# Two blocks of a language model on one core: evictions and weight splits in another order, eight products moved into a recurrence

## The reference

```python
y_ssm = mamba2_mixer(z, xbc, dt_raw, ...) @ w_out_ssm      # four groups of 512 channels, each with its norm
y_lru = rglru_mixer(lru_x, lru_y, ...) @ w_out_lru         # 1280 channels, ten blocks of 128
h = h + (g_ssm * y_ssm + g_lru * y_lru) @ w_out            # g = sigmoid gates, 2 x 1024
h = h + (silu(gate) * up) @ w_ffn_out
return rmsnorm(h, norm_f_w)
# in rglru_mixer, per 128 channels:
u = causal_dwconv(xl); r, i = sigmoid(u@w_r + b_r), sigmoid(u@w_i + b_i)
a = exp(-8·r·softplus(-lam)); b = sqrt(-expm1(2·log a))·i·u
h_t = a_t·h_{t-1} + b_t;  out = h · gelu(yl)
```

## Time and profile before

| | |
|---|---|
| median of three runs | 3571.42 us (3570.7 to 3572.22) |
| profiled execution, its own time | 3571.62 us |
| its span | 3569.5 us |
| PE busy / DVE busy / ACT busy | 94% / 48% / 37% |
| granted TensorE clock, mean | 0.978 of 2.4 GHz |
| HBM read | 282.64 MB, 80 GB/s over the span |

### The profile page before, as it was taken

The page is one execution under the profiler, slowest core; times in us unless marked ns, Lnnn a source line. Parts: engine busy times, 40 slices in busy tenths (PEclk is TensorE's granted clock), DMA queues, the critical chain, the costliest instruction groups (busy, mean ns, idle before and its releaser), DMA issues.

```text
span 3569.5 us, 38933 instructions
## 1 busy us (share of the span) xinstructions
PE 3362.7 (94%) x15366; PEld 2724.7 (76%) x15366; DVE 1722.0 (48%) x2415; ACT 1334.0 (37%) x1894; POOL 30.6 (1%) x62
## 2 busy tenths in 40 slices
PE   8999989899999999998989999989998998999998
PEld 6888766677888888876667788877777876778887
DVE  4443444754443444344575444455445566544443
ACT  4332335343332333233534332345444456433322
POOL 0000000000000000000000000000000000000000
PEclk9999999999999999999999999999999999999999
DMA  4233211112333233321111223321211222333332
GB/s 141 95 97 94 93 65 53 33 54 89 97 94 99 91 99 92 98 90 59 59 33 60 88 96 92 99 70 45 74 48 48 84 84 69 96 97 100 95 93 67
DMA packets 107396, 288.05 MB, mean 81 GB/s; under 512 B 22912, under 2 KB 34176, under 8 KB 107216
## 3 DMA queue, kind: packets, MB, share of 16 engines
q1 hardware_dynamic: 91696, 278.70, 25.0%
q10 hardware_dynamic: 14208, 2.63, 0.4%
q0 software_dynamic: 1312, 4.25, 0.4%
HBM read 282.64 MB, written 2.88 MB: 80 GB/s over the span
## 4 chain that ended last, share of the span: by engine, by line
PE 76%; DVE 12%; ACT 8%; issue 3%; ACTq 1%; DMA 1%; DVEq 0%; SPq 0%
PE ps L729 23%; PE ps L731 22%; PE ps L730 22%; DVE wl L1841 3%; ACT wh L1298 3%; DVE mf L2025 2%; PE ps L738 2%; PE ps L1038 1%; PE ps L1033 1%; PE ps L1194 1%; DVE mf L2035 1%; PE ps L1176 1%; PE ps L1190 0%; ACTq L1575 0%; PE ps L743 0%
## 5 line engine op out<-in xcount | busy, mean ns | idle before, releaser
L1841 DVE TENSOR_TENSOR wl<-raw,wh 128x1024 fp32r<-128x1024 f32 (+2 forms) x581 | 652.5, 1123 | 1448.0 <-ACT wh L1298 1446.2
L729 PE MATMUL ps<-hnh,wh 128*128 128x512 f32 x2712 | 1095.7, 404 | 38.4 <-DVE mf L2488 12.7
L730 PE MATMUL ps<-hnl,wh 128*128 128x512 f32 x2712 | 1070.6, 395 | 0.0
L731 PE MATMUL ps<-hnh,wl 128*128 128x512 f32 x2712 | 1070.1, 395 | 0.0
L1298 ACT ACTIVATE wh<-raw 128x1024 fp32r<-128x1024 f32 (+2 forms) x581 | 567.4, 977 | 1055.9 <-PE ps L731 1024.8
L729 PEld LDWEIGHTS ps<-hnh,wh 128*128 128x128 f32 x2712 | 519.3, 191 | 170.4 <-issue 24.5
L731 PEld LDWEIGHTS ps<-hnh,wl 128*128 128x128 f32 x2712 | 518.0, 191 | 111.4
L730 PEld LDWEIGHTS ps<-hnl,wh 128*128 128x128 f32 x2712 | 519.6, 192 | 108.3 <-issue 4.0
L729 PE MATMUL ps<-mr,wh 128*128 128x512 f32 x1300 | 511.7, 394 | 18.6 <-DVE h L1967 8.2
L731 PE MATMUL ps<-mr,wl 128*128 128x512 f32 x1300 | 507.0, 390 | 0.0
L730 PE MATMUL ps<-mr,wh 128*128 128x512 f32 x1300 | 506.8, 390 | 0.0
(11 more groups left out here) (324 smaller groups left out, 2533.0 us busy)
## 6 DMA issues: line engine op xcount, KB each, us to landing
raw<-in_w_in SPq DMA_DIRECT2D x140, 512.0 KB, 3.5
raw<-in_ffn_w_gate SPq DMA_DIRECT2D x88, 512.0 KB, 3.5
raw<-in_ffn_w_up SPq DMA_DIRECT2D x88, 512.0 KB, 3.5
raw<-in_ffn_w_down SPq DMA_DIRECT2D x64, 512.0 KB, 3.5
raw<-in_w_ffn_in SPq DMA_DIRECT2D x44, 512.0 KB, 3.5
raw<-in_ffn_w_down SPq DMA_DIRECT2D x32, 384.0 KB, 3.1
raw<-in_w_out SPq DMA_DIRECT2D x32, 256.0 KB, 2.6
raw<-in_w_out_ssm SPq DMA_DIRECT2D x32, 256.0 KB, 2.6
```

Of the source, the lines that this page charges most:

```text
L729: self.e.matmul(out, ah, bh, start=start, stop=False, skip_group_check=shared)
L730: self.e.matmul(out, ah, bl, start=False, stop=False, skip_group_check=shared)
L731: m = self.e.matmul(out, al, bh, start=False, stop=stop, skip_group_check=shared)
L1841: self.e.tensor_tensor(lo[:, 0:n], k.raw[u % NRAW][:, 0:n], hi[:, 0:n].bitcast(F), ALU.subtract).then_inc(k.w_lo, 1)
```

## The change

Four edits. In `Vector`, `split` only notes the unit, and the instruction is issued by `flush`, which stands at the start of each step, unit and product and behind the evictions of `add_h`, `ffn_up` and `take_mix`. In `Program`, `rstd` on PE only notes that rows are due, and `root_rows` issues them two steps (6 matmuls) into the next product; where the stage's products are short, the first sum also moves behind the next product. The eight products of the last group go from ahead of `lru` into its iterations 1 to 3, the gate products from iterations 1 and 3 to 3 and 4, and slots in SBUF are dealt out anew. The table of `ssm_heads` has 45 steps in place of 43, with paces some 5% up, and 0.6 in place of 0.65 in `lru`.

```diff
-PACE_SSM_ROWS, PACE_SSM, PACE_LRU, PACE_LRU_END = 1.1, (1.1, 0.82, 0.82, 0.9), 0.65, 1.0
+PACE_SSM_ROWS, PACE_SSM, PACE_LRU, PACE_LRU_END = 1.1, (1.15, 0.86, 0.86, 0.95), 0.6, 1.0
+LRU_OUT, LRU_GATE = ((), (0, 1, 2), (3, 4, 5), (6, 7), ()), {3: 4, 4: 5}
-AT_CB, AT_TURN, AT_X = (0, 2, 2, 3), (6, 8), 8
-AT_ARG, AT_EXP, AT_W, AT_V = 6, 7, 8, 12
+AT_CB, AT_TURN, AT_X = (0, 2, 2, 3), (6, 10), (8, 9, 12, 13)
+AT_ARG, AT_EXP, AT_W, AT_V = 8, 9, 10, 14
...
 class Program:
     def step(self):
+        self.flush()
...
     def product(self, xs, ready, bank=None):
-        for _ in self.pieces(xs, ready, bank):
+        for n, _ in enumerate(self.pieces(xs, ready, bank)):
             self.beside()
+            if n == 1:
+                self.root_rows()
...
     def run_late(self):
-            if i >= 6:
-                self.sums(i - 6)
+            if i == 6 and not self.short:
+                self.sums(0)
             if i == 7:
+                if self.short:
+                    self.sums(0)
+                self.sums(1)
...
     def second(self, gain):
-        self.pace = 0.0
-        self.ssm_out(3)
         self.lru(gain)
...
     def lru(self, gain):
             for i in range(2):
                 self.product_h()
                 self.end_taps()
                 self.taps = self.lru_conv(p, i, u[i])
+                if outs:
+                    self.ssm_out_tile(3, outs.pop(0))
...
-            if p in (1, 3):
-                self.branch_acc(4 + p // 2)
+            for i in outs:
+                self.ssm_out_tile(3, i)
+            if p in LRU_GATE:
+                self.branch_acc(LRU_GATE[p])
...
 class Tensor:
     def rstd(self):
-        self.wait_ge(*k.rs_v.at(self.rs_n(), "cols"))
-        self.rows_of(k.ps[B_RSTD], k.rc, k.rs_p.up(self.rs_n(), "rows"))
+        self.rows_due = self.rs_n()
+    def root_rows(self):
+        k, n = self.k, self.rows_due
+        if n is not None:
+            self.rows_due = None
+            self.wait_ge(*k.rs_v.at(n, "cols"))
+            self.rows_of(k.ps[B_RSTD], k.rc, k.rs_p.up(n, "rows"))
...
 class Vector:
     def split(self, u):
+        self.flush()
+        self.unsplit = u
+    def flush(self):
+        if self.unsplit is not None:
+            u, self.unsplit = self.unsplit, None
+            self.split_unit(u)
+    def begin_product(self, bank):
+        self.flush()
+    def begin_unit(self):
+        self.flush()
...
     def add_h(self, i, scale):
                                     op0=ALU.mult, op1=ALU.add).then_inc(k.took, 1)
+        self.flush()
```

More of the change, by code:

```diff
@@ L182, in __init__ @@
         self.g_v = steps("g_v", in_order(
-            [(AT_X + i, f"x{i}") for i in range(4)], [(AT_ST + 2 + 4 * c, f"{n}{c}") for c in (1, 2) for n in "ds"],
+            four_at("x", AT_X), [(AT_ST + 2 + 4 * c, f"{n}{c}") for c in (1, 2) for n in "ds"],
             [(AT_OFF + 1 + 4 * c, f"m{c}") for c in range(1, 4)], [(AT_Y + 4 * c, f"y{c}") for c in range(1, 4)],
@@ L297, in __init__ @@
         self.gates_done, self.prepared = {}, []
+        self.short, self.rows_due, self.unsplit = False, None, None
         self.qk_took, self.v_took = {}, {}
@@ L345, in split @@
         pass
+    def flush(self):
+        pass
     def pieces(self, xs, ready, bank=None):
@@ L417, in add_h_all @@
         self.r += 1
+        self.short = len(xs) < 8
         for i in range(8):
@@ L655, in ssm_out, with ssm_out_tile @@
     def ssm_out(self, g):
+        for i in range(8):
+            self.ssm_out_tile(g, i)
+    def ssm_out_tile(self, g, i):
         k = self.k
[L657 to L660, removed]
+        xs = [k.pair(S_X[g % 2] + j, S_LO + j) for j in range(4)]
+        b = self.product(xs, lambda j: (k.g_a.at(g, f"hi{j}"), k.g_v.at(g, f"lo{j}")))
+        self.take_out(g, i, b)
         self.out_unit[g] = self.u
@@ L665, in lru @@
         self.lam()
-        y = [k.pair(L_Y + 2 * i, L_Y + 2 * i + 1) for i in range(10)]
+        y = [k.pair(s, s + 1) for at in L_Y for s in (at, at + 2)]
         uh = [k.pair(L_UH + 2 * i, L_UH + 2 * i + 1) for i in range(2)]
@@ L693, in lru @@
         gate = [k.slot(n) for n in L_GATE]
-        parts = [k.pair(L_UH + i, L_LO[i]) for i in range(8)]
+        parts = [k.pair(L_HI[i], L_LO[i]) for i in range(8)]
         for i in range(8):
@@ L1814, in scans @@
                     self.wait_ge(*V.at(p, f"y{i}"))
+                    if p >= 2:
+                        self.wait_ge(*k.acc_v.at((3, 3, 5)[p - 2], "set"))
+                    if p >= 3:
+                        self.wait_ge(k.unit_done, self.out_unit[3])
                     e.activation(y[2 * p + i][0][:, :], u[i][:, :], ACT.Copy).then_inc(*A.up(p, f"hi{i}"))
@@ L1835, in split, with flush, split_unit @@
     def split(self, u):
+        self.flush()
+        self.unsplit = u
+    def flush(self):
+        if self.unsplit is not None:
[5 more added lines that the diff above has]
+        self.flush()
+    def split_unit(self, u):
         k = self.k
@@ L1848, in start @@
         self.hn_last = 0
-        self.split(0)
+        self.split_unit(0)
         self.wait_ge(k.loaded["col"], 16)
@@ L1853, in start @@
             if i == 1:
-                self.split(1)
+                self.split_unit(1)
             self.wait_ge(*k.hn_a.at(i, "hi"))
@@ L1862, in start @@
             if i in (5, 7):
-                self.split((i - 1) // 2)
+                self.split_unit((i - 1) // 2)
         self.wait_ge(k.loaded["cst"], 32)
@@ L2382, in take_branch @@
         self.taken()
-        if n < 8:
-            self.wait_ge(self.k.unit_done, self.out_unit[2])
+        if n < 4:
+            self.wait_ge(*self.k.g_p.at(3, "n2"))
+        elif n < 8:
+            self.wait_ge(self.k.unit_done, self.out_unit[3])
         self.e.tensor_tensor(d[:, :], self.bank()[:, :], self.k.rs[:, :], ALU.mult).then_inc(self.k.took, 1)
@@ L2419, in ssm_heads @@
                 self.prepared.append(g)
-            if AT_X <= t < AT_X + 4:
-                i = t - AT_X
+            if t in AT_X:
+                i = AT_X.index(t)
                 bank = (st, off)[i % 2][:, :].rearrange("p (c q e) -> p c q e", c=4, q=2)
@@ L2691, in plan_units @@
             tiles(w, 0, 4)
-    tiles(ins["w_out_ssm_2"][3], 0, 8)
     for p in range(5):
-        tiles(w, 56 + 2 * p, 2)
+        outs = list(LRU_OUT[p])
+        for i in range(2):
+            tiles(w, 56 + 2 * p + i, 1)
+            if outs:
+                tiles(ins["w_out_ssm_2"][3], outs.pop(0), 1)
         tiles(w, 66 + 2 * p, 2)
-        if p in (1, 3):
-            tiles(w, 4 + p // 2, 1)
+        for i in outs:
+            tiles(ins["w_out_ssm_2"][3], i, 1)
+        if p in LRU_GATE:
+            tiles(w, LRU_GATE[p], 1)
         for m in ("lru_w_r_2", "lru_w_i_2"):
```

17 lines of the change are left out of this document (11 added, 6 removed).

## The result

The changed kernel takes 3430.09 us (median of four runs, 3421.9 to 3435.55) against 3571.56 us: a ratio of 0.9602, 95% interval 0.9583 to 0.9622. In a later measurement the same kernel took 3427.41 us.

A forecast was written before the change was run, and what follows sets the result against it. PE, busy for 94% of the span, was taken as the bound, with about 207 us of gaps. Gains of 29 + 20 + 17 + 22 + 9, 97 us, took the median of 3571.4 to 3475 us, range 3442 to 3522.

The forecast's parts named there:

- The prediction's own sign: Whole kernel: a mean granted clock near 0.985 would show the forecast right.
- 17 of 39.8 us, with the clock: State-space groups: deferred splits shorten short waits, 17 us gained including clock and the table's two steps; bounds 8 and 27.
- PE's products hide the steps: State-space table: two more steps help a transposition, within the 17 us, and are worth nothing by themselves elsewhere.
- Mixers' ends: End of each mixer: some 9 of 10.3 us of waits go, clock gives 2; 11 us, twice; bounds 7 and 13 each.
- Attention: Attention and heads: a quarter of 41.3 us of gaps goes, 10 us per layer, 20 in both; bounds 4 and 16 per layer.
- Recurrence: Recurrence: 20.7 us from earlier evictions, 3 from the eight moved products, 5 from clock; 29 us, bounds 15 and 37.
- The rivals' bound: Recurrence becomes DVE's: it cannot go under 190 us; at 210 it gains 9, not 29; total 3495 us, chance 0.10.
- The four other roots: Roots not counted elsewhere: later rows let PE work meanwhile, 5.4 us, with slow pieces 9 us together; bounds 5 and 12.
- Almost all gaps close: Rival, whole kernel: nearly all gaps go with their slow pieces, the upper bounds, 3438 us; chance 0.07.
- The next link: Rival: chains through ACT return the gain at the next wait; half of the sum, 3523 us; chance 0.20.
- DVE's splits come too late: Rival, recurrence and mixer's end: delayed splits cost PE up to 0.68 us each; 3611 us at 200 paid splits; chance 0.03.
- The drain at the mixers' ends: Rival: DVE needs 5.6 us per tile, so order does not matter there; 22 us less gain, 3497 us; chance 0.02.

## Why the prediction missed

**The sign and most of the waits were right, most of the clock was missing.** DVE's idle time ahead of splits fell from 1446 to 603 us; the lone evictions that held PE in the recurrence cost 2.6 us in place of 12.7; feed-forwards kept their length (358.4 us, the dip behind the root gone); PE's wait for the reciprocal is 0.7 us, a little under the 0.8 to 0.9 expected; the granted clock is 0.988. The 141.2 us by which the spans differ can be parted, since both kernels run the same 15366 matmuls: what PE is less idle is waits, and what it is less busy is in the main clock. From the windows (length less PE's busy time) and the two pages:

| stage | PE idle, before and after | idle less | busy less | predicted |
|---|---|---|---|---|
| recurrence | 30.5 and 10.3 | 20.1 | 6.3 | 23.7, and 5 of clock |
| mixers, two | 83.4 and 57.3 | 26.1 | 5.5 | 20, no clock |
| state-space stage | 39.8 and 14.4 | 25.4 | 13.9 | 17 with the clock |
| mixers' ends, two | 20.6 and 0.8 | 19.8 | 12.0 | 18, and 4 of clock |
| all else | 32.5 and 27.0 | 5.5 | 6.6 | 5.4, and 3.4 of clock |
| sum | 206.8 and 109.9 | 96.9 | 44.3 | 97 |

The waits alone gave what the prediction had for waits and clock together, and 44.3 us came on top. By the mean clocks 37 of these are the clock's (0.022 of 3569.5 less 0.012 of 3428.3). The sum names 12.4 us of clock and has an unnamed share in the state-space stage. The prediction's own sign, a mean clock near 0.985, would have been 26 us, 0.022 of 3569.5 less 0.015 of 3475.

**The step that failed: the state-space stage's "17 of 39.8 us, with the clock".** It was 39.3 us, half of what the sum lacked, and beyond the bound of 27. The prediction held the table's two steps and the deferral to be one gain, "which is in the 17 us". They are two, each about as large as the whole term: the table alone takes 16.9 us out of the groups; the deferral alone takes 3.5 us ahead of the groups and 17.1 in them, together 20.6. The waits for L2428 were in the trace of before, 9.8 us in five, and the table alone ends them; I had looked at L1200, whose steps keep their distance in the table. The prediction named a transposition (L743, 4.5 us of these) and held that for all else in the table "PE's products hide the steps". The states (L1228, 5.3 us) wait for the same L2428, and PE stood still for both: the products that could have hidden the wait are written behind it. And the paces alone add 9.6 us to the window, so it is the places that gain.

**Mixers' ends: the term was mis-sized.** I took 11 us for each, and 15.4 and 16.4 came (14.4 for the first from matmul to matmul). The parts are deferral 9.6 and 10.3, rows and sums 6.1 and 7.8, and together nearly their sum. My working left 1.3 us of waits and half of the clock behind; the rows show PE busy for 42.35 of 42.6 us at clock 1.00: nothing is left. The clock does not simply follow the sum of the waits: in the second end the deferral alone leaves PE idle for 3.0 us at a clock of 0.93, and the rows alone for 7.0 us at 1.00.

**Attention: one chain stood for all, and the clock was left out.** PE's idle time fell by 11.0 and 15.2 us, where I had a quarter of 41.3, 10. The chain that I read, with its 6.59 us, was to get shorter by a fifth; all waits of its kind together went from 19.6 to 9.6 us, and the longest is 3.0. The clock lost 0.04 of 373 us, 15 us, in the first mixer before and 0.05, 19, in the second, and I had a term for it in every stage but this one, though this is the stage with the most time at 1.2 GHz. PE's busy time then fell by 8.2 us in the second layer and rose by 2.7 in the first. With the deferral alone it fell in both, by 7.5 and 6.8 us, and each mixer was 21 us shorter.

**Recurrence: right in size.** 26.4 us for 29. The clock gave 8.8 less 3.9, 5 us, as predicted. The split of the rest was off: the deferral alone took 16.5 us (I had 20.7), the interleaving with its gates and pace some 5 to 6 beside its clock (I had 3). The rivals' bound, 190 us with VectorE as the limit, was not reached: DVE is busy for 138.9 of 192.6 us.

**The four other roots** had 9 us, and all that lies outside the other stages gave 12.

**The rivals.** By its time the result stands nearest to "Almost all gaps close", 3438 us, but they did not: 109.9 of 206.8 us are left, and the two times lie close together because so much came from the clock. The next link did not take over: ACT's tables still stand in attention, but of the waits looked at only that for `wl` grew. "DVE's splits come too late" was real in a small way, 5.0 us in the groups, at a place that I had not named: not where units are short, but where one product uses four units. The drain at the mixers' ends did not show. By my working of the Trainium skill, VectorE: DVE Perf Modes, section The DRAIN you can't avoid, a tile would take 5.6 us; the trace has 3.00, less even than the sum of the four durations, 3.34, since each instruction starts 0.08 to 0.09 us ahead of the recorded end of the one before.

## What to carry to other kernels

On an engine that takes its instructions in order, put what another engine waits for ahead of what has lead, and do it behind every such instruction: splits that were left behind a convolution's taps cost 11 to 14 us of the 3430, with the clock, and PE waited for them for 7 us of that at one place. List every wait of the bottleneck engine in a stage before an edit there is called worth nothing. And where waits go, price the slow clock that goes with them in each stage: here it was some 40 of 141 us.

## What the runs showed of the hardware

Beside the changed kernel's four executions, 3421.9 to 3435.55 us, the kernel before took 3570.7 to 3572.22, and over all the measurements here 3569.18 to 3577.55. The changed kernel's 14 us go with mean granted clocks from 0.991 in the shortest run to 0.986 in the longest. In the first mixer of its two profiled executions PE was granted 1.2 GHz for one stretch of 13.7 us, 180 us in, and for one of 3.4 us at the same place; the work was the same. So part of the time depends on where the clock falls, and 7 us between two kernels is about as little as four runs can tell here.

ScalarE starts directly behind a table load. In the changed kernel, at the first root:

```profile
390.12 1.28 ACT L1426 ACT_TABLE_LOAD   x1
...
391.41 0.26 ACT L1426 ACTIVATE small<-ps,col 128x4 f32<-128x4 f32 x1
```

390.12 + 1.28 is 391.40. In 98 of the 132 loads of this trace the next instruction starts within 0.1 us of the load's end. The drain of 1.38 us that the Trainium skill, ScalarE: Activation LUTs, section What ACT_TABLE_LOAD costs, puts behind a load does not show here either, and with it the wait of 0.7 us for the reciprocal could not have been so short.
